# First attention in a new order: scores of the next head ahead, sums of squares of six heads in two single-pass matmuls

## The reference, cut to what matters

```python
qkv = rms_norm(h, g_norm) @ w_qkv               # 528 x 3072
q, k = rotary(q), rotary(k)                     # per head two maps of width 64, v of width 128
a = softmax(q1 @ k1.T * scale) - lam * softmax(q2 @ k2.T * scale)     # chunk-causal mask
o = a @ v                                       # one head: 528 x 128
o = rms_norm(o, g_sub) * (1 - lam_init)         # norm over the 128 values of the head
h = h + concat(o) @ w_o
```

## Time and profile before

| what | us |
|---|---|
| median of three runs | 2028.45 |
| the profiled execution | 2028.63 |
| its span in the trace | 2026.80 |
| TensorE busy in the span | 2009.0 |
| VectorE, GpSimd, ScalarE busy | 1317.6, 1164.9, 852.0 |

### The profile page before, as it was taken

How to read it: one execution, slowest core, us unless ns; L and a number is a source line. 1 busy time by engine, 2 the same in 40 slices (tenths; PEclk the granted TensorE clock), 3 DMA queues, 4 the chain that set the end, 5 groups by cost and what they waited for, 6 DMA issues and landing times.

```text
span 2026.8 us, 37421 instructions
## 1 busy us (share of the span) xinstructions
PE 2009.0 (99%) x13376; PEld 1804.8 (89%) x13376; DVE 1317.6 (65%) x2199; ACT 852.0 (42%) x1499; POOL 1164.9 (57%) x1395
## 2 busy tenths in 40 slices
PE   9999999999999999999999999999999999999998
PEld 9999899999999988899999998777788888988987
DVE  7777757857746868757857778865512457857654
ACT  5444434433423577634433425344422234433433
POOL 6445356675757522146675767744455557766765
PEclk9999999999999999999999999999999999999999
DMA  5222122232233311122232323322223223232322
GB/s 190 84 74 72 53 85 92 84 117 92 92 97 115 94 34 42 32 89 94 67 131 94 104 94 105 104 84 83 74 93 103 84 84 95 83 125 83 125 83 84
DMA packets 51986, 183.06 MB, mean 90 GB/s; under 512 B 5648, under 2 KB 7824, under 8 KB 51856
## 3 DMA queue, kind: packets, MB, share of 16 engines
q1 hardware_dynamic: 50304, 178.87, 27.3%
q10 hardware_dynamic: 1552, 2.42, 0.4%
HBM read 179.17 MB, written 2.10 MB: 89 GB/s over the span
## 4 chain that ended last, share of the span: by engine, by line
PE 93%; DVE 4%; issue 1%; ACT 1%; POOL 1%; DMA 0%; DVEq 0%; ACTq 0%; SPq 0%
PE ps L805 25%; PE ps L806 24%; PE ps L807 24%; PE ps L929 3%; PE ps L930 3%; PE ps L931 3%; PE ps L1180 2%; PE ps L1197 1%; PE ps L1190 1%; PE ps L1090 1%; PE ps L1121 1%; POOL w_lo L759 1%; PE ps L1105 0%; PE ps L1191 0%; PE ps L1407 0%
## 5 line engine op out<-in xcount | busy, mean ns | idle before, releaser
L739 POOL TENSOR_TENSOR w_lo<-w_raw,w_hi 128x256 fp32r<-128x256 f32 x1140 | 964.1, 878 | 744.5 <-ACT w_hi L2256 735.9
L805 PE MATMUL ps<-x_hi,w_hi 128*128 128x264 f32 (+2 forms) x2504 | 823.0, 329 | 0.0
L806 PE MATMUL ps<-x_lo,w_hi 128*128 128x264 f32 (+2 forms) x2504 | 813.5, 325 | 0.0
L807 PE MATMUL ps<-x_hi,w_lo 128*128 128x264 f32 (+2 forms) x2504 | 812.3, 324 | 0.0
L805 PEld LDWEIGHTS ps<-x_hi,w_hi 128*128 128x128 f32 x2504 | 471.3, 188 | 49.6 <-issue 5.4
L806 PEld LDWEIGHTS ps<-x_lo,w_hi 128*128 128x128 f32 x2504 | 470.8, 188 | 42.1 <-issue 0.2
L807 PEld LDWEIGHTS ps<-x_hi,w_lo 128*128 128x128 f32 x2504 | 471.3, 188 | 39.6
L2256 ACT ACTIVATE w_hi<-w_raw 128x1024 fp32r<-128x1024 f32 x267 | 278.0, 1049 | 72.1 <-PE ps L807 56.4
L805 PE MATMUL ps<-g_hi,w_hi 128*128 128x264 f32 (+3 forms) x648 | 207.9, 321 | 1.0 <-DVE g_lo L1916 1.0
L806 PE MATMUL ps<-g_lo,w_hi 128*128 128x264 f32 (+3 forms) x648 | 205.9, 318 | 0.0
L807 PE MATMUL ps<-g_hi,w_lo 128*128 128x264 f32 (+3 forms) x648 | 205.6, 317 | 0.0
(11 more groups left out here) (278 smaller groups left out, 3044.1 us busy)
## 6 DMA issues: line engine op xcount, KB each, us to landing
w_raw<-stream SPq DMA_DIRECT2D x334, 512.0 KB, 3.5
h<-x_t SPq DMA_DIRECT2D x4, 528.0 KB, 6.7
out_t<-h SPq DMA_DIRECT2D x6, 256.0 KB, 2.3
scratch<-rotary_tables ACTq DMA_DIRECT2D x4, 264.0 KB, 5.4
out_t<-h ACTq DMA_DIRECT2D x2, 256.0 KB, 2.5
par<-params ACTq DMA_DIRECT2D x1, 342.0 KB, 4.7
scratch<-positions ACTq DMA_DIRECT2D x1, 256.0 KB, 2.6
cst<-shape_constants ACTq DMA_DIRECT2D x1, 193.0 KB, 6.2
```

The lines of the kernel that those rows point to most:

```text
L739: last = nc.gpsimd.tensor_tensor(w_lo[:, ring(j), cols], w_raw[:, j % 4, cols], w_hi[:, ring(j), cols].bitcast(F32), ALU.subtract)
L805: nc.tensor.matmul(out_ap, w_hi[:, s, c], xh[:, k, cols], start=first, stop=False)
L806: nc.tensor.matmul(out_ap, w_hi[:, s, c], xl[:, k, cols], start=False, stop=False)
L807: return nc.tensor.matmul(out_ap, w_lo[:, s, c], xh[:, k, cols], start=False, stop=last)
```

## The change

The sums of squares of heads 0 to 5 are no longer taken by a float32 matmul. ScalarE copies the squares into `sum_hi` (fp32r) after unit 3, GpSimd subtracts to get `sum_lo`, and TensorE multiplies both with the ones, two single passes per bank. TensorE issues scores 1 to 4 of the next head ahead of the sum and the value transposes. ScalarE's order in a head becomes: `take_transposed` of unit 0, then exponentials 2 and `take_transposed` 1, and so on; exponentials 1 of the next head stand ahead of `take_values`. VectorE's norm steps go behind `combine` and the piece. GpSimd's loop over low parts is written out by head, with the subtraction behind the third of four. In the last head the output blocks are spread otherwise, and two more of them stand ahead of the last norm. In the second attention the scores of unit 4 use 128 query columns where they used 16. The diff, without the two semaphores and the arguments that carry `held` and a pair of banks; lines with ... mark what is left out:

```diff
@@ -730,10 +732,10 @@
 def _(pool):
-    def lo_part(j, i=0, ordered=True):
-        pool.wait_ge(hi_ready, j + 1 + 4 * i)
+    def lo_part(j, i=0, ordered=True, stride=4):
+        pool.wait_ge(hi_ready, j + 1 + stride * i)
         if ordered:
-            wait(pool, half_done, j - 3 + 4 * i)
+            wait(pool, half_done, j - 3 + stride * i)
@@ -774,9 +776,27 @@
     first_lo_part()
-    for j in range(1, 4):
+    def head_sum_low(n, par_):
...
+        pool.wait_ge(head_sum_hi, n + 1)
+        nc.gpsimd.tensor_tensor(sum_lo, sq[:, par_, :], sum_hi.bitcast(F32),
+                                ALU.subtract).then_inc(head_sum_lo, 1)
...
+    def head_tiles(hd, par_, j, i=0):
...
+        for m in range(3):
+            lo_part(j + m, i, stride=8)
+        head_sum_low(hd - 1, 1 - par_)
+        lo_part(j + 3, i, stride=8)
...
+    for j in range(1, 11):
         lo_part(j)
-    begun = 4
+    head_tiles(1, 1, 11)
+    with pool.Fori(0, (HEADS_A - 4) // 2) as i:
+        for n in range(2):
+            head_tiles(2 * i + 2 + n, n, 15 + 4 * n, i)
+    head_tiles(HEADS_A - 2, 0, 31)
+    begun = 4 * (HEADS_A - 2) + 11
@@ -830,7 +850,7 @@
-    def tile_pair(j, tl, blocks, xh, xl, T, ready, begun=False):
+    def tile_pair(j, tl, blocks, xh, xl, T, ready, begun=False, held=2):
@@ -839,12 +859,12 @@
             for bank, t0, n in chunks(T):
-                for b in range(blocks - 1 - m, blocks):
+                for b in range(blocks - (held if m else 1), blocks):
...
-    def tiles(j, tl, n, blocks, xh, xl, T, ready, after_first=None, paired=False, begun=False, T_odd=None):
+    def tiles(j, tl, n, blocks, xh, xl, T, ready, after_first=None, paired=False, begun=False, T_odd=None, held=2):
@@ -1173,11 +1194,11 @@
             wait(pe, o_taken_b, 5 * (h - 2) + 2)
-        s = scores_b(idx)
+        s = scores_b(idx) if t else ps[:, 4, UNIT_COLS[2] + UNIT_COLS[3]:UNIT_COLS[2] + UNIT_COLS[3] + META]
...
                 wait(pe, o_taken_b, 5 * (h - 1))
-            last = nc.tensor.matmul(s[:, k0:k1], q_b[rows, h % 4, q0:q0 + nq], k_b[rows, h % 4, k0:k1],
+            last = nc.tensor.matmul(s[:, k0:k1], q_b[rows, h % 4, q0:q0 + P], k_b[rows, h % 4, k0:k1],
@@ -1243,11 +1264,22 @@
-    def sub_sum(n, par_, bank0=0, pieces=0):
+    def sub_sum(n, par_, bank0=(0, 1), pieces=0):
...
+    def sub_sum_of_parts(n, pieces):
...
+        pe.wait_ge(r_ready, N_SUB + n)
+        pe.wait_ge(head_sum_lo, n + 1)
+        for bank, t0, width in chunks(T1):
+            pe.wait_ge(chunk_taken, pieces + bank)
+            out_ap = ps[:, bank, 0:width]
+            nc.tensor.matmul(out_ap, ones[:, :].bitcast(F32R), sum_hi[:, t0:t0 + width], start=True, stop=False)
+            last = nc.tensor.matmul(out_ap, ones[:, :].bitcast(F32R), sum_lo[:, t0:t0 + width], start=False, stop=True)
+        last.then_inc(ss_ready, 1)
...
     def wo_blocks(m, n, b0, b1):
@@ -1256,8 +1288,6 @@
         def step(f, idx):
...
-        for idx in range(1, 5):
-            step(scores, idx)
@@ -1266,36 +1296,39 @@
                 piece_a(hd + 1, 4)
+        for idx in range(1, 5):
+            scores(hd + 1, 1 - par_, idx)
         if sums:
-            sub_sum(hd - 1, 1 - par_, 0, 6 * hd + 11)
+            sub_sum_of_parts(hd - 1, 6 * hd + 11)
...
     def last_head_a():
         hd, par_ = HEADS_A - 1, 1
-        for idx in range(1, 5):
-            scores(hd, par_, idx)
         transposes(hd, par_, 0)
-        sub_sum(HEADS_A - 2, 0)
+        pe.wait_ge(ln_done, N_SUB + HEADS_A - 2)
+        wo_blocks(0, 0, 0, 5)
         values(hd, par_, 0)
+        pe.wait_ge(exp_done, 5 * hd + 2)
+        sub_sum(HEADS_A - 2, 0, (2, 5))
         transposes(hd, par_, 1)
-        pe.wait_ge(ln_done, N_SUB + HEADS_A - 1)
-        wo_blocks(0, 0, 0, 5)
+        wo_blocks(0, 1, 0, 5)
...
         transposes(hd, par_, 2)
-        wo_blocks(0, 1, 0, 5)
+        wo_blocks(0, 0, 5, 6), wo_blocks(0, 1, 5, 6)
...
         transposes(hd, par_, 3)
-        wo_blocks(0, 0, 5, 6), wo_blocks(0, 1, 5, 6)
+        wo_blocks(0, 0, 6, 7), wo_blocks(0, 1, 6, 7)
...
         transposes(hd, par_, 4)
-        wo_blocks(0, 0, 6, 7), wo_blocks(0, 1, 6, 7)
+        pe.wait_ge(ln_done, N_SUB + HEADS_A - 1)
+        wo_blocks(1, 0, 0, 2)
...
         pe.wait_ge(r_ready, N_SUB + HEADS_A - 1)
-        wo_blocks(1, 0, 0, 3)
-        sub_sum(HEADS_A - 1, 1, 4)
-        wo_blocks(1, 0, 3, 6), wo_blocks(1, 1, 0, 6)
+        wo_blocks(1, 0, 2, 6)
+        sub_sum(HEADS_A - 1, 1, (4, 5))
+        wo_blocks(1, 1, 0, 7), wo_blocks(1, 0, 6, 7)
@@ -1312,6 +1345,8 @@
     piece_a(0, 5)
+    for idx in range(1, 5):
+        scores(0, 0, idx)
@@ -1323,7 +1358,7 @@
     last_head_a()
-    tiles(J_WO, TL_WO, KD, KD, g_hi, g_lo, T1, (g_ready, G_WO), paired=True, begun=True)
+    tiles(J_WO, TL_WO, KD, KD, g_hi, g_lo, T1, (g_ready, G_WO), paired=True, begun=True, held=1)
@@ -1921,10 +1956,10 @@
         for idx in range(4):
+            combine(hd, par_, idx + 1)
+            piece_a(hd + 1, 1 - par_, idx)
...
                 (sub_scale, sub_hi, sub_lo)[idx](hd - 2)
-            combine(hd, par_, idx + 1)
-            piece_a(hd + 1, 1 - par_, idx)
@@ -1937,18 +1972,17 @@
             maximum(hd, par_, idx)
+        combine(hd, par_, 1)
         sub_scale(hd - 2)
-        combine(hd, par_, 1)
         take_output(hd, par_, 0)
+        combine(hd, par_, 2)
         sub_hi(hd - 2), sub_lo(hd - 2)
-        combine(hd, par_, 2)
         take_output(hd, par_, 1)
+        combine(hd, par_, 3)
         sub_scale(hd - 1)
-        combine(hd, par_, 3)
         take_output(hd, par_, 2)
-        sub_hi(hd - 1)
         combine(hd, par_, 4)
-        sub_lo(hd - 1)
+        sub_hi(hd - 1), sub_lo(hd - 1)
@@ -2459,25 +2494,28 @@
     def sub_square(n, par_):
...
-    def sub_rms(n, bank0=0):
+    def sub_rms(n, banks=(0, 1)):
         wait(act, sub_step, n)
-        inverse_rms(N_SUB + n, P, T1, acc, bank0)
+        inverse_rms(N_SUB + n, P, T1, acc, banks)
     def head_a(hd, par_, j, i=0):
...
         for idx in range(5):
+            if idx in range(1, 4):
+                exps(hd, par_, idx + 1)
+            take_transposed(hd, par_, idx)
             if idx == 4:
-                take_transposed(hd, par_, idx)
                 exps(hd + 1, 1 - par_, 0)
-            else:
-                exps(hd, par_, idx + 1)
-                take_transposed(hd, par_, idx)
...
                 hi_part(j + 3 + (0, None, 1, 2, 3)[idx], i, 8)
+            if sums and idx == 3:
+                act.wait_ge(sq_ready, SQ[N_SUB] + hd)
+                A.activation(sum_hi, sq[:, 1 - par_, :], ACT.Copy).then_inc(head_sum_hi, 1)
+        exps(hd + 1, 1 - par_, 1)
@@ -2487,12 +2525,14 @@
     def last_head_a():
         hd, par_ = HEADS_A - 1, 1
-        exps(hd, par_, 1)
         take_transposed(hd, par_, 0)
-        sub_rms(hd - 1)
-        for idx in range(1, 4):
-            exps(hd, par_, idx + 1)
-            take_transposed(hd, par_, idx)
+        exps(hd, par_, 2)
+        sub_rms(hd - 1, (2, 5))
+        take_transposed(hd, par_, 1)
+        exps(hd, par_, 3)
+        take_transposed(hd, par_, 2)
+        exps(hd, par_, 4)
+        take_transposed(hd, par_, 3)
...
     def take_group(n):
@@ -2609,6 +2649,7 @@
     hi_part(6)
+    exps(0, 0, 1)
@@ -2619,7 +2660,7 @@
     sub_square(HEADS_A - 1, 1)
-    sub_rms(HEADS_A - 1, 4)
+    sub_rms(HEADS_A - 1, (4, 5))
```

More of the change, by code:

```diff
@@ L516, in program @@
         u_copied = sem("u_copied")
+        head_sum_hi = sem("head_sum_hi")
+        head_sum_lo = sem("head_sum_lo")
         post_step = sem("post_step")
@@ L855, in tiles @@
                 if paired:
-                    tile_pair(j, tl, blocks, xh, xl, T, ready, begun)
+                    tile_pair(j, tl, blocks, xh, xl, T, ready, begun, held)
                     done = 2
@@ L872, in norm_sum @@
             def norm_sum(steps, T, src=acc, semaphore=acc_step, bank0=6, pieces=0):
+                banks = bank0 if isinstance(bank0, tuple) else (bank0, bank0 + 1)
                 pe.wait_ge(semaphore, steps)
@@ L876, in norm_sum @@
                     wait(pe, chunk_taken, pieces + bank if not isinstance(pieces, int) or pieces else 0)
-                    last = nc.tensor.matmul(ps[:, bank0 + bank, 0:n], ones[:, :], src[:, t0:t0 + n],
+                    last = nc.tensor.matmul(ps[:, banks[bank], 0:n], ones[:, :], src[:, t0:t0 + n],
                                             start=True, stop=True)
@@ L2319, in inverse_rms @@
                     act.wait_ge(ss_ready, norm + 1)
-                    src = ps[:, bank0, 0:T2] if T == T2 else ps[:, bank0:bank0 + 2, 0:T // 2]
+                    a, b = bank0 if isinstance(bank0, tuple) else (bank0, bank0 + 1)
+                    src = ps[:, a, 0:T2] if T == T2 else ps[:, a:b + 1:b - a, 0:T // 2]
                 else:
```

## The result

The changed kernel takes **2060.22 us**, the median of 5 runs (2059.13 to 2064.51), beside 2028.07 of the kernel before in as many runs: ratio 1.0161, 95% interval 1.0146 to 1.0176. The profiled execution took 2060.22, its span is 2058.4. The forecast was 2043.0, with a range up to 2049. The sign and the place are as forecast, the size is not: +31.6 us of span, where the sum had +14.4.

A forecast was written before the change was run, and what follows sets the result against it. TensorE, one stream of matmuls, was taken as the bound. Boundaries +19.4, waits -3.2, last head -0.2 and second attention -1.6 summed to +14.4 us, giving 2043.0 us (75%), overall range 2037.5 to 2049.

The forecast's parts named there:

- The sign and the place: A loss, +14.4 us, at the head boundaries of the first attention; slower was given 93%.
- the boundary chain: Head boundaries: `combine`, maximum 1, exponentials 1, then `take_values` delay the next head's first transposes; +19.4 us over eight boundaries.
- V + 5.78: First transposes of the next head (T0) start 5.78 us after the last values are issued (V); before, 3.44.
- rival 2: Idle 2.8 us at eight boundaries makes TensorE's clock fall, 2.5 us each: +20, 2063 us; 8%.
- 2.8 alone should pass: Idle 2.8 us at a boundary leaves the clock at 1.00, judged from 3.3 us idle at the trace's end.
- The waits on `combine`: TensorE's wait on `combine` of unit 1 goes, 0.65 us in each of heads 2 to 6: -3.2 us.
- The sums: Heads 0 to 5: 0.50 us instead of 1.10 each, the 0.60 gain worth nothing within the idle time.
- the subtraction and the copy: GpSimd's subtraction and ScalarE's copy to `sum_hi` for the sums: done in time, cost 0.
- piece 0 and the logarithm: The next head's piece 0 waits for the logarithm behind `take_values`, ready about when the transposes end: 0, bound +1 us.
- rival 1: Boundary chain covered, first transposes at V + 2.95: a gain of 9.3 us, 2019 us; 5%.
- The last head: First transposes to first matmul behind the last norm, 20.93 us before: -0.2 us, bounds -2 and +2.
- Second attention: Unit 4's scores with full-width weight loads gain 0.1 us in each of 16: -1.6 us, bounds -2 and +1.

The follow-up runs named there:

- experiment 1: The changed kernel with ScalarE's `take_values` ahead of the exponentials of unit 1 at every head boundary: 2044.72 us, ratio 1.0074.
- experiment 9: The changed kernel with `take_values` and the norm's logarithm and exponential ahead of the exponentials of unit 1 on ScalarE: 2031.3 us, ratio 1.0009.
- experiment 6: The kernel before with only ScalarE's exponentials of unit 1 of the next head moved ahead of `take_values`: 2062.83 us, ratio 1.0167.
- experiment 2: The changed kernel with 14 unread matmuls of 256 columns at each of eight boundaries, value transposes ahead of them and the sum: 2051.34 us.
- experiment 4: The changed kernel with the sums of squares of heads 0 to 5 as plain float32 matmuls again: 2056.14 us, ratio 1.0134.
- experiment 7: The changed kernel with `take_values` ahead of exponentials 1, and TensorE's order scores 1, value transposes, sum, scores 2 to 4: 2051.1 us.
- experiment 10: experiment 7 with the norm's logarithm and exponential also ahead of exponentials 1, and the last head's output blocks reordered: 2021.44 us, ratio 0.9965.
- experiment 12: experiment 10 with the scores of unit 4 in the second attention back on 16 query columns: 2021.77 us.
- with seven matmuls: experiment 2 with 7 instead of 14 unread matmuls at each boundary: 2056.23 us.

## Why the prediction was wrong, and where it was right

**Right: the boundary chain.** V + 5.78 was forecast; three of seven boundaries have 5.75 to 5.76, one 5.95. Experiments 1 and 9, which take the exponentials of unit 1 out of the chain, show it to be the cause, and experiment 6 shows that it needs nothing else of the change. The total is +21.2 instead of +19.4, because three boundaries have 6.3 to 6.5. In those the multiply inside `combine` took 1.03 us where it takes 0.50 elsewhere, each time with GpSimd's low part starting 0.01 us after it (more on this at the end). In 6.49 and 5.95 there are 0.2 more between the end of `take_values` and T0 (0.25 where it is 0.05 elsewhere), for a reason that stays open.

**Wrong: rival 2 was no rival but a part of the forecast.** The step that failed reads: "2.8 alone should pass". By it the sum has no term for the clock at all, and puts at nothing what took 10.3 us in seven heads and about 2 more in the last. It rested on the end of the trace, where the clock is 1.00 through 3.3 us without a matmul and 0.50 after the earlier trace rows. From the one stretch in which it held I took that an idle 2.8 us is harmless; but the same rows show it at half directly behind. The idle pieces were of the forecast length where the multiply was quick (2.66 three times), and the clock fell at each of them. Filled idle time and an unmoved chain give 10.3 us in the seven heads (experiment 2). The price inside the rival was wrong too: 2.5 us a fall, from the start of the kernel, where a stretch of 3.4 us costs 1.1 to 1.5. Its 2063 lies near the measured 2060 partly by luck: the chain and the waits came near, 1.8 more of boundary, 4 of the last head, and seven falls at 1.1 to 2.6 in the heads before, not eight at 2.5. The Trainium skill ("TensorE: Matmul & The Clock Gate", "HAM oscillation — how this bites in real kernels") warns of idle gaps between bursts that throw the clock back each time; this trace agrees, with nine falls.

**The waits on `combine`:** -3.2 forecast, -2.8 in experiment 2. Right.

**The sums:** priced at 0.50, they take 0.61 to 0.66, and in the kernel before up to 0.90. That they are worth nothing under the new chain was right, and even generous: experiment 4 is faster without them. That the subtraction and the copy cost nothing was right; no wait in the changed kernel names them.

**Taken at 0, bound +1: piece 0 and the logarithm.** In the changed kernel this held, since the chain ahead of it is longer. It is the term that made rival 1 impossible: with `take_values` first, the logarithm is next in line, 1.9 us in experiment 1 and 3.0 in experiment 7. Rival 1 also had T0 at V + 2.95, the end of the value transposes, as if `take_values` could be done by then. With TensorE's order of the change it reads their result, and the best seen in a head with a sum is V + 3.93 (experiments 1 and 9), 0.5 later than before.

**The last head:** forecast -0.2. From T0 to the first matmul behind the last norm it takes 24.93 (258.34 to 283.27) instead of 20.93, +4.0. The wait before blocks 6 and 7 came as worked out (2.4, forecast 2.7), but two falls of the clock, 10.2 us at half speed, lie at its start and in it. In experiment 2, which has only the second of them, it takes 22.93: the first costs 2.0. If the second costs 1.1 to 1.5 as elsewhere, an estimated 0.5 to 0.9 over before is left, where -0.2 was forecast. With both gone and the blocks reordered it takes 20.13 (experiment 10).

**Second attention:** forecast -1.6, measured -1.0 by landmarks, and 0.9 in experiment 12. By the Trainium skill's rule on weight loads ("TensorE: Matmul & The Clock Gate", "LDWEIGHTS (loading the stationary operand)") it would have been an estimated +3; the landmarks of both pairs of traces, 1.0 and 0.9 us less, speak against that.

## What to carry to other kernels

Before a block is moved ahead of another on an in-order engine, list all that is queued behind it and who waits for each: here it was `take_values`, then the logarithm, and moving only the first past the block shifted the wait and kept most of the loss. Idle time of TensorE between bursts costs twice, as waiting and as matmuls at half clock behind it, so price a new wait with both, and look at the granted clock behind the idle stretch. A cheaper step beside a longer wait is worth nothing or less; repair the order first, then count it (2.5 us here).

## What was not expected of the hardware

- Idle time in pieces is no protection: in experiment 1 0.83 and 1.77 us with 0.8 us of transposes between were followed by 0.50, in experiment 9 the first of the two alone was not. Nor is it a rule: in experiment 1 itself 1.04 and 1.94 us at the boundary into the last head were followed by no fall.
- Useless matmuls paid: 112 of them made the kernel 8.9 us faster.
- The same VectorE multiply of 128 x 528 float32, in the changed kernel, with GpSimd's subtraction starting 0.01 us after it and 0.17 us after it:

```profile
97.47 1.03 DVE L1857 TENSOR_SCALAR scratch<-scratch,small 128x528 f32<-128x528 f32 x1
97.48 3.44 POOL L741 TENSOR_TENSOR w_lo<-w_raw,w_hi 128x256 fp32r<-128x256 f32 x4 [3.78 <-ACT w_hi L2290]
...
129.15 0.50 DVE L1857 TENSOR_SCALAR scratch<-scratch,small 128x528 f32<-128x528 f32 x1
129.32 3.41 POOL L741 TENSOR_TENSOR w_lo<-w_raw,w_hi 128x256 fp32r<-128x256 f32 x4 [3.92 <-ACT w_hi L2290]
```

Both multiplies overlap the subtraction, so that running side by side does not double the time; what differs is how close the two starts are. In all 14 traces such a multiply takes 1.03 or 1.04 us where the subtraction starts 0.01 or 0.02 us behind it, and 0.49 or 0.50 where it starts 0.08 us or more behind. The first kind comes three times in each of the twelve kernels that have GpSimd's new loop (64.68, 97.47 and 252.77 us in the changed one), and never in the kernel before and in experiment 6, which have the old one. So the change itself brought these three, about 0.5 us each in the chain, and the forecast had no term for them. Moving the start alone was not tried.

What decides between falls of 3.4 and 6.8 us stays open, and so does why of boundaries with the same idle time one fell and one did not: 2.27 us in experiment 4 at 132.67 (no fall), 162.41 and 193.44 (falls), with seven matmuls 3.13 us at 69.80 (none) beside 1.90 at 160.36 (a fall), and in experiment 6 3.26 us at 169.21 (none) beside the same at 104.03 and 137.17 (falls).
